# A transposed residual stream and a weight-stationary output projection in a two-layer hybrid decoder step

## The reference

```python
def rmsnorm(x, g):
    return x * rsqrt(mean(x * x, -1) + EPS) * g

for l in range(2):
    mk, mv = split(rmsnorm(mem_prompt, g_mem[l]) @ w_mem_kv[l])      # 256 memory rows
    p = rmsnorm(x, g_mix_norm[l]) @ w_in[l]
    u, v, xb, q = split(p)                       # widths 384, 384, 384, 256
    a = gelu(u) * (w_spatial @ rmsnorm(gelu(v), g_v) + b_spatial)
    b = (trailing_means(xb) - xb) @ w_pool * s_pool
    o = softmax(q @ k.T / 8) @ v_mem             # 4 heads of 64, memory of 256
    x = x + concat(rmsnorm(a), rmsnorm(b), rmsnorm(o)) * g_group @ w_out[l]
    h = rmsnorm(x, g_ffn_norm[l])
    if l == 0:
        x = x + (silu(h @ w_gate) * (h @ w_up)) @ w_down             # width 2816
    else:                                        # top 2 of 8 experts, width 3584
        gates = top2_softmax(h @ w_router)
        x = x + sum(gates[:, e] * ((silu(h @ wg[e]) * (h @ wu[e])) @ wd[e]) for e in range(8))
y = rmsnorm(x, g_final)
```

## Time and profile before

| | |
|---|---|
| median of 3 runs | 1564.09 us (1563.2 to 1570.7) |
| the profiled execution | 1566.53 us, its span 1564.8 us |
| mean granted clock of PE | 0.982 of 2.4 GHz |
| busy: PE, DVE, ACT, POOL | 1478.5, 1164.8, 956.1, 81.8 us |
| chain that ended last | PE 86%, DVE 6%, ACT 4%, issue 2%, POOL 1% |
| DMA | 456.83 MB, mean 292 GB/s over the span |

### The profile page before, as it was taken

How to read it: one execution, slowest core, us unless ns; L and a number is a source line. 1 busy time by engine, 2 the same in 40 slices (tenths; PEclk the granted TensorE clock), 3 DMA queues, 4 the chain that set the end, 5 groups by cost and what they waited for, 6 DMA issues and landing times.

```text
span 1564.8 us, 21548 instructions
## 1 busy us (share of the span) xinstructions
PE 1478.5 (94%) x7632; PEld 1239.8 (79%) x7632; DVE 1164.8 (74%) x1058; ACT 956.1 (61%) x925; POOL 81.8 (5%) x107
## 2 busy tenths in 40 slices
PE   4899899999799869999999999999999999999996
PEld 3687699999788657888888888888888887888774
DVE  3635455544455368889898898889888889889997
ACT  4434354333344247777777777777777777777774
POOL 2001000000201030000000000000000000001011
PEclk9999999999899979999999999999999999999999
DMA  8445577542442239999999999999999999999992
GB/s 338 150 148 176 175 246 245 195 169 101 189 167 96 81 142 362 367 362 391 360 368 398 365 368 390 370 365 386 374 374 383 363 370 380 364 365 359 406 388 83
DMA packets 77097, 456.83 MB, mean 292 GB/s; under 512 B 7649, under 2 KB 20863, under 8 KB 25455
## 3 DMA queue, kind: packets, MB, share of 16 engines
q1 hardware_dynamic: 73086, 442.64, 75.4%
q10 hardware_dynamic: 2016, 7.34, 1.1%
q0 software_dynamic: 1952, 6.28, 1.0%
HBM read 434.63 MB, written 21.88 MB: 292 GB/s over the span
## 4 chain that ended last, share of the span: by engine, by line
PE 86%; DVE 6%; ACT 4%; issue 2%; POOL 1%; ACTq 0%; DMA 0%; DVEq 0%; POOLq 0%; SPq 0%
PE bank L309 28%; PE bank L311 27%; PE bank L310 27%; ACT whi L293 2%; DVE wlo L297 2%; PE bank L1644 2%; PE bank L1291 1%; ACT junk L519 1%; DVE hT_lo L803 1%; DVE x L1138 0%; DVE xn L796 0%; PE bank L1417 0%; ACT hT_hi L528 0%; POOL rstd L419 0%; PE bank L1622 0%
## 5 line engine op out<-in xcount | busy, mean ns | idle before, releaser
L297 DVE TENSOR_TENSOR wlo<-raw,whi 128x2048 fp32r<-128x2048 f32 x402 | 920.7, 2292 | 203.3 <-ACT whi L293 191.8
L293 ACT ACTIVATE whi<-raw 128x2048 fp32r<-128x2048 f32 x402 | 768.9, 1915 | 162.7 <-PE bank L311 162.3
L309 PE MATMUL bank<-whi,gT_hi 128*128 128x512 f32 x896 | 363.8, 406 | 1.8 <-DVE gT_lo L1143 1.8
L310 PE MATMUL bank<-wlo,gT_hi 128*128 128x512 f32 x896 | 353.3, 394 | 0.0
L311 PE MATMUL bank<-whi,gT_lo 128*128 128x512 f32 x896 | 352.7, 394 | 0.0
L311 PEld LDWEIGHTS bank<-whi,gT_lo 128*128 128x128 f32 x896 | 168.8, 188 | 39.6
L309 PEld LDWEIGHTS bank<-whi,gT_hi 128*128 128x128 f32 x896 | 168.7, 188 | 35.7 <-issue 2.0
L310 PEld LDWEIGHTS bank<-wlo,gT_hi 128*128 128x128 f32 x896 | 169.3, 189 | 34.1
L309 PE MATMUL bank<-whi,eT_hi 128*128 128x512 f32 x448 | 174.8, 390 | 1.9 <-DVE eT_lo L1158 1.9
L311 PE MATMUL bank<-whi,eT_lo 128*128 128x512 f32 x448 | 175.2, 391 | 0.0
L310 PE MATMUL bank<-wlo,eT_hi 128*128 128x512 f32 x448 | 174.6, 390 | 0.0
(11 more groups left out here) (220 smaller groups left out, 1462.4 us busy)
## 6 DMA issues: line engine op xcount, KB each, us to landing
raw<-in_stream SPq DMA_DIRECT2D x402, 1024.0 KB, 7.0
x_slots<-zero SPq DMA_DIRECT2D x18, 640.0 KB, 9.7
rows_e<-x_slots ACTq DMA_DIRECT2D x7, 512.0 KB, 7.7
y_slots<-y_rows ACTq DMA_DIRECT2D x7, 512.0 KB, 8.6
table<-in_table SPq DMA_DIRECT2D x2, 896.0 KB, 14.4
const<-in_const SPq DMA_DIRECT2D x1, 1192.0 KB, 21.6
stage<-in_mem SPq DMA_DIRECT2D x2, 512.0 KB, 3.8
x<-in_x_prompt SPq DMA_DIRECT2D x1, 1024.0 KB, 10.8
```

Source lines behind the costliest of these rows:

```text
L293: nc.scalar.activation(whi[:, slot % SPL, :], raw[:, slot, :], ACT.Copy).then_inc(hi_ready, 1)
L297: nc.vector.tensor_tensor(wlo[:, slot % SPL, :], raw[:, slot, :], whi[:, slot % SPL, :].bitcast(F), ALU.subtract).then_inc(lo_ready, 1)
L309: nc.tensor.matmul(out, a_hi, b_hi, start=start, stop=False, **kw)
L310: nc.tensor.matmul(out, a_hi, b_lo, start=False, stop=False, **kw)
```

## The change

- The residual lives as `xT`, [128, 8 blocks, 288 tokens], from the opening up to the router. PE turns x once at the start; the output projection and the dense down product give their outputs transposed and are added to `xT` block by block. `hT_hi` and `hT_lo` come from `xT` times the gain alone (`hi_of_x`, `lo_of_x`), with no turning and no row factor.
- The row factor rstd goes to the products' outputs: as scale of Gelu and of the eviction of xb (tokens on partitions), and for outputs with tokens along the free axis as `rB`, rstd spread over all partitions by a matmul of ones with a diagonal (`spread_rstd`), multiplied into q and into the gate and up blocks (`gs`, `us`; Silu is then taken of `gs`). The router's logits stay unscaled; rstd enters `nfirst` and the scale of Exp.
- The sum of squares of x: ACT squares each block, POOL adds the blocks up in `ssum` (`power_of_x`), PE sums over partitions (`sums_of_x`), DVE makes mean and diagonal, POOL the power.
- Memory rows are turned once, unscaled; both layers' hi and lo parts come from that copy (`mem_hi_of`, `mem_lo_of`), the factor is applied when keys and values are evicted. The turns of x ride between the products of layer 1's keys and values.
- The output projection has the weights stationary and the 288 tokens moving, in eight banks.
- PE turns `xT` back to rows ahead of the experts (24 transposes), ACT copies them to `x`.
- The zero fills go from SP's queue to POOL's, one after each used `up` chunk; `table` and `state` of layer 1 too, behind the sum of squares and the zeroing of `qs` and `xn`. SP waits once for a memset ahead of x_sample and no longer for `zero_set` and `x_dense`.
- SBUF places of the tiles change; the expert loop's instructions do not.

```diff
-            sp.wait_ge(S["zero_set"], 1)
             with nc.sync.Fori(0, UP_CH // RAWS) as i:
                 for j in range(RAWS):
                     c = C_UP + RAWS * i + j
                     load_chunk(sp, (c, c), (C_UP + j) % RAWS)
-                    fill(sp, x_slots[bass.ds((RAWS * i + j) * FILL, FILL), :], FILL)
...
-            sp.wait_ge(S["x_dense"], KD + 2)
-            sp.dma_start(table[:, :], io["table"][1]).then_inc(table_in, 16)
-            sp.dma_start(state[:, :], io["state"][1]).then_inc(state_in, 16)
...
+            def power_of_x(u, n):
+
+                for k in range(KD):
+                    pool.wait_ge(sq_out, KD * u + k + 1)
+                    if k:
+                        nc.gpsimd.tensor_tensor(ssum[:, 0:NT], ssum[:, 0:NT], sq[:, k % 2, :], ALU.add)\
+                            .then_inc(ssum_out, 1)
+                        pool.wait_ge(ssum_out, (KD - 1) * u + k)
+                pool.wait_ge(ms_out, u + 1)
+                nc.gpsimd.tensor_tensor(rstd[:, n, :], ms[:, n, :], half[:, :], ALU.pow).then_inc(rstd_ok, 1)
...
+                    power_of_x(1, N_MIX)
+                    zero_pair(qs)
                     nc.gpsimd.memset(xn[:, 2, :], 0.0).then_inc(S["xn_blank"], 1)
-                    zero_pair(qs)
-
-                pool.wait_ge(table_in, 16 * (l + 1))
+                    pool.dma_start(table[:, :], io["table"][1]).then_inc(table_in[1], 16)
+                    pool.dma_start(state[:, :], io["state"][1]).then_inc(state_in[1], 16)
...
+                power_of_x(2 * l, N_FFN)
+                if l == 0:
+                    pool.wait_ge(S["zero_set"], 2)
+                    for n in range(FILLS - 2):
+                        pool.wait_ge(chunk_used, C_UP + 1 + n)
+                        fill(pool, x_slots[n * FILL:(n + 1) * FILL, :], FILL)
+                    fill(pool, x_slots[NE * SLOTS - FILL_LEFT:NE * SLOTS, :], FILL_LEFT)
+                    fill(pool, y_slots[Y_ROWS:Y_ROWS + P, :], P)
...
+            def hi_of_x(l, which, *blocks):
+
+                for k in blocks:
+                    nc.scalar.activation(hT_hi[:, k, :], xT[:, k, :], ACT.Copy,
+                                         scale=gains[:, l, which, k:k + 1]).then_inc(hx_hi, 1)
+
+            def square_of_x(u, k):
+
+                if k == 0 and u:
+                    act.wait_ge(ss_done, u)
+                if k == 0:
+                    act.wait_ge(S["zero_set"], 2)
+                if k > 2:
+                    act.wait_ge(ssum_out, (KD - 1) * u + k - 2)
+                nc.scalar.activation(sq[:, k % 2, :] if k else ssum[:, 0:NT], xT[:, k, :], ACT.Square).then_inc(sq_out, 1)
...
+                for k in range(4):
+                    act.wait_ge(S["x_mixed"], KD * l + k + 1)
+                    square_of_x(2 * l, k)
...
-                act.wait_ge(S["x_mixed"], 6 * l + 3)
-                sum_squares(x[:, :, 0:512], N_FFN, signal=False)
+                act.wait_ge(chunk_used, c0 + 15)
+                hi_of_x(l, G_FFN, 0, 1, 2, 3)
                 if l == 0:
                     hi_static(act, C_UP + 1)
-                for t in range(3):
-                    act.wait_ge(S["x_mixed"], 6 * l + 4 + t)
-                    sum_squares(x[:, :, 512:D], N_FFN2, (t,), signal=t > 0)
-                turn_hi(l, G_FFN, NT)
+                for k in (4, 5, 6):
+                    act.wait_ge(S["x_mixed"], KD * l + k + 1)
+                    square_of_x(2 * l, k)
+                act.wait_ge(chunk_used, c0 + 16)
+                hi_of_x(l, G_FFN, 4, 5, 6)
+                act.wait_ge(S["x_mixed"], KD * l + KD)
+                hi_of_x(l, G_FFN, 7)
+                square_of_x(2 * l, 7)
...
+                    for m in range(KD // 2):
+                        hi_static(act, C_DOWN + 3 * m + 3)
+                        for j in (2 * m, 2 * m + 1):
+                            act.wait_ge(S["x_dense"], j + 3)
+                            hi_of_x(1, G_MIX, j)
+                            square_of_x(1, j)
+                            if j % 2 == 0 or m < 3:
+                                hi_static(act, C_DOWN + 3 * m + 4 + j % 2)
...
+            def lo_of_x(l, which, *blocks):
+
+                for k in blocks:
+                    dve.wait_ge(hx_hi, times(l, which == G_FFN) + k + 1)
+                    V.scalar_tensor_tensor(out=hT_lo[:, k, :], in0=xT[:, k, :], scalar=gains[:, l, which, k:k + 1],
+                                           in1=hT_hi[:, k, :].bitcast(F), op0=ALU.mult, op1=ALU.subtract).then_inc(hx_lo, 1)
+
+            def mean_of_x(u, n, b):
+
+                dve.wait_ge(ss_done, u + 1)
+                V.tensor_scalar(ms[:, n, :], bank[b][:, 0:6].rearrange("p (t a) -> p t a", a=2)[:, :, 0], 1.0 / D, EPS,
+                                ALU.mult, ALU.add).then_inc(ms_out, 1)
+
+            def spread_rstd(l, e, n):
+
+                dve.wait_ge(rstd_ok, rstd_event(l, e))
+                for t in range(3):
+                    last = V.tensor_scalar(diag[:, t * P:t * P + ROWS[t]], ident[:, 0:ROWS[t]], rstd[:, n, t:t + 1], None,
+                                           ALU.mult)
+                last.then_inc(diag_out, 1)
+
+            def keep_rB(n_th, b):
+
+                dve.wait_ge(rB_done, n_th)
+                V.tensor_copy(rB[:, :], bank[b][:, 0:NT]).then_inc(rB_out, 1)
...
+                    mean_of_x(1, N_MIX, 0)
+                    spread_rstd(1, E_MIX, N_MIX)
+                    keep_rB(3, 1)
 
                 dve.wait_ge(chunk_used, c0 + 3)
-                dve.wait_ge(zeroed, 2 * l + 1)
+                dve.wait_ge(rB_out, 2 * l + 1)
                 for f in range(2):
-                    last = V.tensor_scalar(qT[:, f, :], bank[4 + f][:, 0:SEQ], HD ** -0.5, None, ALU.mult)
+                    last = V.scalar_tensor_tensor(out=qT[:, f, :], in0=bank[4 + f][:, 0:NT], scalar=HD ** -0.5,
+                                                  in1=rB[:, :], op0=ALU.mult, op1=ALU.mult)
...
+                def mixed(k):
+
+                    if k == 0:
                         dve.wait_ge(chunk_used, c0 + 14)
+                    if k >= 4:
+                        dve.wait_ge(S["block_done"], 4 * l + k - 3)
+                    V.tensor_tensor(xT[:, k, :], xT[:, k, :], bank[(2, 3, 4, 5, 6, 7, 0, 1)[k]][:, 0:NT], ALU.add)\
+                        .then_inc(S["x_mixed"], 1)
+                    dve.wait_ge(S["x_mixed"], KD * l + k + 1)
+                for k in range(4):
+                    mixed(k)
                 if l == 0:
+                    lo_static(dve, C_UP)
+                lo_of_x(l, G_FFN, 0, 1, 2, 3)
+                mixed(4)
+                mixed(5)
+                if l == 0:
+                    lo_static(dve, C_UP + 1)
+                mixed(6)
+                mixed(7)
+                lo_of_x(l, G_FFN, 4, 5, 6, 7)
+                if l == 0:
+                    mean_of_x(0, N_FFN, 0)
+                    lo_static(dve, C_UP + 2)
+                    spread_rstd(0, E_FFN, N_FFN)
+                    keep_rB(2, 1)
+                    dve.wait_ge(stored, 16 * (MEM_STORES + LAYER_STORES))
+                    dve.wait_ge(rB_out, 2)
...
+                            V.tensor_tensor(xT[:, j, :], xT[:, j, :], bank[6 + j % 2][:, 0:NT], ALU.add)\
+                                .then_inc(S["x_dense"], 1)
+                            lo_of_x(1, G_MIX, j)
...
+            def sums_of_x(u, b):
+
+                pe.wait_ge(ssum_out, (KD - 1) * (u + 1))
+                for t in range(3):
+                    last = T.matmul(bank[b][:, 2 * t:2 * t + 2], ssum[:, t * P:(t + 1) * P], ones[:, 0:2],
+                                    start=True, stop=True)
+                last.then_inc(ss_done, 1)
+
+            def spread_rstd(n_th, b):
+
+                pe.wait_ge(diag_out, n_th)
+                T.matmul(bank[b][:, 0:NT], ones, diag[:, :], start=True, stop=True).then_inc(rB_done, 1)
...
-                def project(n, k, tiles=(0, 1, 2)):
-
-                    c = c0 + 12 + 2 * n + k // 4
-                    for t in tiles:
-                        r = ROWS[t]
-                        m = mm3(bank[2 + 3 * n + t][0:r, :], hT_hi[:, k, t * P:t * P + r], hT_lo[:, k, t * P:t * P + r],
-                                blk(whi, c, 4 * (k % 4), 4), blk(wlo, c, 4 * (k % 4), 4), k == 0, k == KD - 1)
+                def project(k, *ds):
+
+                    for d in ds:
+                        c = c0 + 12 + d // 4 * 2 + k // 4
+                        m = mm3(bank[(2, 3, 4, 5, 6, 7, 0, 1)[d]][:, 0:NT], blk(whi, c, 4 * (k % 4) + d % 4),
+                                blk(wlo, c, 4 * (k % 4) + d % 4), hT_hi[:, k, :], hT_lo[:, k, :], k == 0, k == KD - 1)
...
+            for t in range(3):
+                for n in range(2):
+                    for k in range(4 * n, 4 * n + 4):
+                        last = T.transpose(bank[ROW_BANKS[2 * t + n]][0:ROWS[t], (k % 4) * P:(k % 4 + 1) * P],
```

(16 more changed lines are left out.)

532 lines of the change are left out of this document (267 added, 265 removed).

## The result

The changed kernel took 1538.76 us (median of 4 runs, 1537.47 to 1540.39), the kernel before, run beside it, 1566.77 (4 runs, 1563.2 to 1570.7). The ratio is 0.982, 95% interval 0.9805 to 0.9842: 28 us or 1.8% less, where 64.6 us were forecast. 1500 us was too low, and 1538.76 lies above the range of 1486 to 1520. The profiled execution took 1538.45 us, its span 1536.7.

The account below looks back on a forecast made before the run. PE was taken to set the length of the expert loop and fill the dense part, leaving gains in projections and joins. Stage gains summed to 64.6 us, from 1566.5 to 1501.9, or 1500 for the median; range 1486 to 1520.

Parts of the forecast that it names:

- The opening: Start to 67.13 us: turning unscaled memory early lets products start at 14.0, queries end at 52.0; gain 15.1, bounds 11 and 18.
- the first attention: 67.13 to 143.33 us: only one of two splits ahead of the sample scores is taken out; gain 1.3 us.
- The projection: Output projection: 192 matmuls with stationary weights replace 144, 1.3 us of waiting; gain 6.6 and 6.5, bounds 5 and 8 each.
- The join ahead of the dense part: 17.66 us between projection and dense part: row scalings and turns gone, first up block costs 6.4; gain 11.3, bounds 8 and 12.
- The layer-1 table: Load by POOL behind the dense part: issued T+12, 14.4 us to land, wanted about T+56, so no cost.
- the dense part: Dense feed-forward, 207.45 us: turns removed, sum, spreading and one 1.7 us wait added; gain 0.3, bounds +2.8 and -4.
- the expert loop: 568.84 to 1564.80 us: PE sets its length and its instructions stay, so 996 us remain after the change.
- the join behind the dense part: Last down product to sample scores' products, 28.0 us: scores' chain ends at T+13.7; gain 14.3, bounds 10 and 16.
- the router join: 540.65 to 568.84 us: ends between T+17.0 and T+20.5, taken as 19.0; gain 9.2, bounds 6 and 12.
- B: Rival: new order loses its covers, split pairs stand in the way at three joins and the opening; 1517 us, chance 0.21.
- C: Rival: slower because 20 zero fills move to POOL's queue; at 11.5 us a fill 1580 us, chance 0.04.
- D: Rival: no gain, stationary weights slower and a DMA-fed expert loop takes the rest back; 1560 to 1568 us, chance 0.02.

Follow-up runs that it names:

- e3: Changed kernel with the count for the first down product set ahead of VectorE's hidden blocks and ScalarE's weight split ahead of silu; 1518.86 us.
- e4: Changed kernel with eT_hi and eT_lo put back at the SBUF addresses they had in the kernel before, nothing else; 1532.83 us.
- e5: Changed kernel with the three products that make diag for layer 1 done by ScalarE instead of VectorE; 1535.66 us.
- e11: Changed kernel with early count, split ahead of silu, diag on ScalarE, 128 bytes padding (1497.25 us), plus gathered rows' tile 1 moved from GpSimd to VectorE; 1495.18 us.
- e2: Changed kernel with ScalarE splitting the next weight chunk ahead of silu in the dense up loop, the count left late; 1524.71 us.

## Why the prediction was wrong, step by step

**Right, and at its size.** The opening: first product at 15.43 instead of 14.0 (turning ended at 8.4 where I had 8.3, and the first split weights came 1.4 us late), queries done at 53.20 instead of 52; with the first attention 15.5 us of 16.4. The projection: 30.62 and 30.21 us, forecast 30, though with 2.1 and 2.8 us of waiting for the 1.3 of the sum. The join ahead of the dense part: 10.9 of 11.3, no wait for the sum's chain. The layer-1 table on POOL's queue landed in 5.0 us and held nothing up; the two loads of before had 14.4.

**The step that failed** is in the dense part: "Each block asks 4.6 us of DVE in 6.4 of PE, so it stays ahead." The 4.6 us are right and the conclusion, an overlap without loss, is not. I added up one engine's work and did not follow the chain through ScalarE, whose silu had until then been fed by PE and is now fed by DVE. The ring takes 6.66 us a block. The same sentence hid the second fault: since DVE "stays ahead", I gave the increment behind the hidden loop no price. Together they cost 19.9 us (e3), of the 20.6 that are missing there.

**A term that was missing:** the expert loop, forecast at the 996 us that it took before. The instructions are unchanged, and I listed "the loop grows" among what would prove me wrong, without giving it a mechanism or a chance. The change moves tiles, and that cost 6.5 us (e4 gives back 5.9; the rest is within the loop's spread).

**Mis-sized: the join behind the dense part**, 14.3 forecast, 8.9 measured. The chain up to POOL's power was right to 0.4 us. I put the zero fills behind the power and priced only when they end, not what they do to the three products for diag beside them: diag came 4.8 us late (T+11.8 for T+7.0), of which 3.9 in the stage and 3.1 in the total come back with ScalarE (e5). I had used that very collision at the router, one paragraph on. It was also the first of my signs of being wrong: PE waiting for the sum's chain in a join.

**Mis-sized: the router join**, 9.2 forecast, 7.7 measured. The rule of the Trainium skill that I weighed and only half took (SBUF — State Buffer, Who interferes with whom) was nearer: T+20.5 by it, 20.51 measured. That the figures meet so closely is chance, for the steps differ: I had the mask wait for both of POOL's operations, while it ended with the first (1.10 us for 0.30), and the 128x1024 product ended 1.1 us behind the second (3.44 for 1.24). With POOL's two operations gone and one product more on DVE, 1.7 us come back (e11).

**The rivals.** B, covers lost, did not happen as told: no split pair stood in the way of a join, and the cover that was lost, behind the dense part, fell to POOL's zero fills. C, zero fills on POOL, did not happen: the page of the changed kernel's profile has 4.3 us from issue to landing for the fills, and one issue took POOL 0.90 us at 169.04 (I had 2.5); POOL's busy time is 24.34 of the dense part's 227.72 us. D is out: PE's projections took the forecast 30 us. None of the bounds covered a loss of 20 us in the dense part (the worst I allowed was 4), and so the range failed (its bounds add up to 1522 and not 1520; 1538.76 is above both). The repairs that were run (e3, e4, e5, e11: 19.9, 5.9, 3.1 and 1.7 us) give back 31 of the 36.5 us; the rest stays open.

## What to carry to other kernels

When an operation moves from one engine to another, add up each chain of dependencies that comes back to where it started, through every engine's own order, and compare the ring with the time of the engine that is to set the pace; the busy sums alone say nothing about it. Look at each count that is raised behind a loop and ask who waits for it, even if today it comes early. And write down where tiles lie in memory before and after: here 128 bytes of padding, no part of the change, gave 16 us, as much as the largest gain of the change.

## What the runs showed of the hardware

- TensorE products with eT's 128x128 blocks of 4-byte values stationary and 512 columns start every 0.227 us if the blocks start at a multiple of 256 bytes in SBUF and every 0.233 us if they start 64 or 128 bytes above one. The weight load shows 188 or 189 ns in both cases, so its duration doesn't give it away; the mean of such a product in the list of costliest groups goes from 390 to 395 ns.
- VectorE's three products of 128x128 by a column, 0.90 us alone, took 5.08 us beside three GpSimd memsets in a row (2.01, 2.01 and 0.94 us); ScalarE's same three took 0.91 beside the first of them. It goes the other way too: GpSimd's power on 128x3, 0.88 at 398.80, took 2.77 at 166.30, beside VectorE's split of a chunk at 166.07 (2.28).
- After waits of 11.92 us (the changed kernel) and 5.28 us (e2) TensorE's down products took 72.8 and 72.9 us at a mean granted clock of 0.96, and 70.4 us at 1.00 with no wait ahead of them (e3).
